# Spreading the mLSTM's rows of maxima and stabilisers by products of exact halves, and its first scores half a unit later

## The chip, the cores and the metric

The kernel runs on one core of one Trainium2 chip. The metric is device time in microseconds (us) of one execution; the kernel before takes 904.87 us, the median of three runs. Engines are named as the profile names them: PE is TensorE (PEld its loads of weights), DVE is VectorE, ACT is ScalarE, POOL is GpSimd, SP is SyncE, which issues the DMAs. L1570 is line 1570 of the kernel before.

## The reference, cut to what matters

256 tokens of width 1024 go through a first block (a gated mixer and a mixture of 32 experts) and then through two hybrid layers, each with three kinds of attention side by side. The change touches only the third kind, the mLSTM, which has 4 heads of 64 channels:

```python
m_t = jnp.maximum(inter_log, jnp.max(d_log, axis=-1))     # a running maximum for each token and head
w_intra = jnp.exp(d_log - m_t[..., None])
sc = jnp.einsum('bhtd,bhsd->bhts', qt, kt) * w_intra
num = (jnp.einsum('bhts,bhse->bhte', sc, vt) + ...)
h_t = num / jnp.maximum(jnp.abs(den), jnp.exp(-m_t))[..., None]
```

The kernel does both chunks of 128 tokens at once. With bt the running sum of the log forget gates, it keeps for each head a row of 256 tokens `rg` = input gate less bt, a row `rM` = running maximum of `rg` (from zero), and the stabiliser `rB` = bt + `rM`. Then w_intra[s, t] = exp(rg[s] - rM[t]) for s <= t, and the lower bound of the denominator is exp(-rB[t]).

## The kernel before, in words

The two hybrid layers are written as one function for each engine: `second_pe`, `second_act`, `second_dve`, `second_pool`, `second_sp`. Each is a hand-written list of steps; nothing reorders them, and the engines meet only through semaphores. The order of the lines at the end of each function is therefore the order on its engine.

The projections of a layer are cut into 22 units of 256 columns. Unit u of a layer is two `tile` steps on PE, `tile(l, u, 0)` and `tile(l, u, 1)`, each of 24 matmuls of 256 columns: 8 slices of the contraction, times 3 products. The 3 products are those of float32 numbers that have been split into two halves of type fp32r: high by high, low by high, high by low. ACT makes the high half of a unit's weights by a copy (`high(l, u)`, L1353) and DVE the low half by a subtraction (`low(l, u)`, L1361), in pieces of 128x1024. Units for values are done with the tokens as weights in `by_token` (L1495, 512 columns each, 48 matmuls for two units). SP loads the unit U when PE is done with unit U-4.

Between the tiles stand the small steps of the attentions, in plain float32. Those of the mLSTM, in PE's order:

```python
tile(l, 6, 0)
stabilisers(l)
tile(l, 6, 1)
m_rows(l, 0)
m_scores(l, 0)
tile(l, 7, 0)
m_rows(l, 1)
tile(l, 7, 1)
m_out(l, 0)
m_scores(l, 1)
```

- `gate_chain` (DVE) makes the rows `rg`, `rM`, `rB`, each 4 partitions (one a head) by 256 tokens. `s_gate` counts its steps.
- `stabilisers` (PE): two tiny matmuls that turn `rg` into columns (L1558, L1559), and two float32 matmuls that spread the rows `rB` over 64 partitions a head (L1561, L1562) by constants `selp` of zeros and ones. ACT takes exp(-.) of them in `stab_exp` (L1822).
- `m_rows(l, j)` (PE, L1570): two float32 matmuls with the constants `selm`, which spread the rows `rM` of heads 2j and 2j+1 over 128 partitions each. DVE's `m_log` (L2065, L2066) subtracts them from a mask into X1, ACT's `m_exp` (L1829) takes the exponential.
- `m_scores(l, j)` (PE, L1584): the products of keys and queries. DVE's `m_weigh` (L2074) multiplies them by X1 into X2.
- `m_out(l, j)` (PE, L1603, L1608): numerator and denominator. ACT's `m_den` (L1833) and DVE's `m_norm` (L2081, L2084, L2087) finish them.

Around these, `conv_silu` (ACT, L1806) ends the mLSTM's convolution, whose taps are DVE's (`taps`, L2008); `gate(l, "co")` (L1870) is a sigmoid; `gate_columns` (L2043) copies the columns of `rg`. Later on PE come `r_scores` (L1621), `norm_mean` (L1645) and `by_token(l, U_AV)`. `r_scores` waits for `m_norm` of heads 2 and 3, `norm_mean` for `m_gate` (L2093), and `by_token(l, U_AV)` for the low halves of the first pieces of units 10 and 11, of which the second is `low(l, 11, 0)`. The constants `selm` and `selp` lie in `late`, a tile that one DMA loads (L2455).

Of the kernel before, what the change touches and what calls it, by code (L numbers as in the profile page):

```python
# [13 lines left out]
T = 256  # L14
# [44 lines left out]
def build(nc, p, out):  # L59
    pe, act, dve, pool, sp = nc.tensor, nc.scalar, nc.vector, nc.gpsimd, nc.sync  # L60
    with ExitStack() as ctx:
        def sb(name, *shape):
            return ctx.enter_context(nc.sbuf_tensor(name, [128, *shape], F32))
# [6 lines left out]
        def overlay(**shapes):  # L70

            with ExitStack() as side:
                return [side.enter_context(nc.sbuf_tensor(n, [128, *shape], F32)) for n, shape in shapes.items()]
# [14 lines left out]
        X1 = sb("X1", 3, 384)  # L88
        rw = sb("rw", 9, 36)
        crep = sb("crep", 8, 32)  # L90
# [3 lines left out]
                                                 X2=(3, 384))  # L94
        (more,) = overlay(more=(2, 4096))
# [15 lines left out]
        def con(name, a=0, n=None):  # L111
            at, w = CONST[name]
            src, at = (cst, at) if at < EARLY else (late, at - EARLY)
            return src[:, at + a:at + (w if n is None else a + n)]
# [1138 lines left out]
        def second_block():  # L1253
# [130 lines left out]
            def root_table():  # L1384

                act.activation(trow[:, 0:1], E6, ACT.Sqrt)
# [58 lines left out]
            def second_pe():  # L1445
# [109 lines left out]
                def stabilisers(l):  # L1555
                    pe.wait_ge(s_late, 16)
                    pe.wait_ge(s_gate, 23 * l + 23)
                    pe.matmul(bank[2][:, 0:4], rg[:, 0:128], ident[0:4, 0:4], start=True, stop=True)  # L1558
                    pe.matmul(bank[2][:, 4:8], rg[:, 128:256], ident[0:4, 0:4], start=True, stop=True).then_inc(s_gcT, 1)  # L1559
                    pe.wait_ge(s_rs, 12 if l else 9)  # L1560
                    pe.matmul(bank[6][:, 0:T], con("selp", 0, 128)[0:4, :], rB, start=True, stop=True)  # L1561
                    pe.matmul(bank[6][:, T:2 * T], con("selp", 128, 128)[0:4, :], rB, start=True, stop=True).then_inc(s_stab, 1)  # L1562

                def m_rows(l, j):
                    if j:
                        pe.wait_ge(s_mW, 8 * l + 4)
                    else:
                        pe.wait_ge(s_gc, l + 1)
                    for x in range(2):
                        pe.matmul(bank[2][:, T * x:T * x + T], con("selm", 256 * j + 128 * x, 128)[0:4, :], rM,  # L1570
                                  start=True, stop=True).then_inc(s_mM, 1)
# [127 lines left out]
                for l in range(2):  # L1699
# [30 lines left out]
                    m_scores(l, 0)  # L1730
                    tile(l, 7, 0)
                    m_rows(l, 1)
                    tile(l, 7, 1)
# [60 lines left out]
            def second_act():  # L1794
# [13 lines left out]
                def gate_start(l):  # L1808
                    act.wait_ge(s_gate, 23 * l + 4)
                    act.activation(ra, rf, ACT.Abs).then_inc(s_gabs, 1)  # L1810
                    act.wait_ge(s_gabs, 2 * l + 1)
                    act.activation(re, ra, ACT.Exp, scale=-1.0).then_inc(s_gabs, 1)
# [70 lines left out]

                root_table()
                for l in range(2):
# [13 lines left out]
                    gate_start(l)  # L1899
                    for j in range(4):  # L1900
                        conv(l, j)
                    high(l, 6)
                    by_token(l, bcv, U_BV, s_bcv)
                    high(l, 7)
                    for j in range(4):
                        conv_silu(l, j)
# [89 lines left out]
            def second_dve():  # L1996
# [15 lines left out]
                def gate_chain(l):  # L2012
                    g, U = 23 * l, NU * l + U_ROWS
# [8 lines left out]
                    dve.wait_ge(s_gabs, 2 * l + 2)  # L2022
# [16 lines left out]
                    yield  # L2039

# [232 lines left out]
                for l in range(2):  # L2273
# [32 lines left out]
                    for j in range(4):  # L2306
                        take(tap[j], 1)
                    gate_columns(l)
                    low(l, 7, 0)
                    for j in range(4):  # L2310
                        take(tap[j], 1)
                    low(l, 7)
# [267 lines left out]
```

## Time and profile before

| | |
|---|---|
| time, median of 3 runs | 904.87 us (904.82 to 905.17) |
| time of the profiled execution | 905.45 us |
| its span in the profile | 904.2 us |
| PE busy | 857.6 us, 95% |
| DVE, ACT busy | 415.3 us, 300.2 us |
| TensorE clock granted | 0.99 of full speed |

The span is the time from the first to the last instruction in the profile; 1.25 us of the execution lie outside it. The first 600 us are the first block, where the experts' weights stream in; the two hybrid layers take the rest, about 152 us each. Everything that the change touches lies between 613 and 665 us (first layer) and 765 and 817 us (second layer).

### The profile page before, as it was taken

What the parts mean: (1) busy time and instruction counts of PE and PEld (TensorE: products, weight loads), DVE (VectorE), ACT (ScalarE), POOL (GpSimd) and SP (SyncE); (2) the same over time, 40 slices, a digit from 0 to 9 for tenths busy, and PEclk for the clock granted to TensorE, in tenths of its full rate; (3) what the DMA queues carried; (4) which work ended last, traced back from release to release, by engine and by line L of the source; (5) the groups of instructions that cost most, each with busy time, mean ns of one, the idle gap of its engine ahead of it and who ended that gap; (6) DMA issues with size and microseconds to landing.
All of it is one profiled execution on the core that took longest, in us unless ns stands there. A gap on an engine that the chain in (4) does not pass through costs nothing.

```text
span 904.2 us, 12189 instructions
## 1 busy us (share of the span) xinstructions
PE 857.6 (95%) x5030; PEld 552.6 (61%) x5030; DVE 415.3 (46%) x807; ACT 300.2 (33%) x542; POOL 10.3 (1%) x14
## 2 busy tenths in 40 slices
PE   5999999999998989898989899999999999999997
PEld 2668875344444334443444243498879999897995
DVE  3196954111210112011111011089798879989875
ACT  4253242111111111110111011174746666556663
POOL 0001000000000000000000000000100000010000
PEclk9999999999999999999999999999999999999999
DMA  9999989999999999999999999963425345643431
GB/s 370 426 424 428 394 349 416 399 428 428 427 427 429 428 427 426 427 429 428 427 428 428 428 422 423 392 235 140 148 87 186 141 163 190 185 137 104 178 140 71
DMA packets 34857, 292.96 MB, mean 324 GB/s; under 512 B 11376, under 2 KB 11888, under 8 KB 12912
## 3 DMA queue, kind: packets, MB, share of 16 engines
q1 hardware_dynamic: 34800, 292.16, 79.2%
q8 instruction: 41, 0.67, 0.3%
q14 instruction: 16, 0.13, 0.0%
HBM read 290.05 MB, written 1.05 MB: 322 GB/s over the span
## 4 chain that ended last, share of the span: by engine, by line
PE 72%; DMA 22%; DVE 4%; ACT 1%; issue 1%; SPq 0%; ACTq 0%
PE bank L1471 20%; PE bank L1019 16%; DMA more<-in_expert_w 14%; PE bank L1050 8%; DMA ring<-in_expert_w 7%; PE bank L1495 5%; PE bank L403 3%; PE bank L1514 2%; PE bank L950 2%; PE bank L419 2%; DVE X L373 2%; PE bank L990 2%; DMA ring<-in_ada_w 2%; PE bank L446 2%; PE bank L1662 1%; PE bank L1688 1%
## 5 line engine op out<-in xcount | busy, mean ns | idle before, releaser
L1019 PE MATMUL bank<-ring,xg 128*64 128x512 f32 x760 | 232.3, 603 | 13.9 <-DMA ring<-in_expert_w 13.9
L1471 PE MATMUL bank<-HH,halves 128*128 128x256 f32 x848 | 163.9, 289 | 0.0
L1019 PEld LDWEIGHTS bank<-ring,xg 128*64 128x64 f32 x760 | 72.7, 139 | 132.3 <-issue 105.9
L1471 PEld LDWEIGHTS bank<-HH,halves 128*128 128x128 f32 x848 | 135.4, 192 | 5.6 <-issue 4.8
L1019 PE MATMUL bank<-more,xg 128*64 128x512 f32 x256 | 116.9, 608 | 7.5 <-DMA more<-in_expert_w 7.5
L1471 PE MATMUL bank<-HL,halves 128*128 128x256 f32 x424 | 120.3, 284 | 0.0
L1137 DVE TENSOR_TENSOR X<-X,bank 128x512 f32<-128x512 f32 x16 | 11.0, 687 | 226.4 <-PE bank L1019 226.4
L1050 PE MATMUL bank<-ring,X 128*64 128x512 f32 x384 | 114.3, 596 | 0.7 <-ACT X L1090 0.7
L1361 DVE TENSOR_TENSOR halves<-raw,halves 128x1024 fp32r<-128x1024 f32 (+1 forms) x84 | 92.0, 1127 | 6.5 <-ACT halves L1353 6.4
L1150 DVE SCALAR_TENSOR_TENSOR ygL<-bank,small,ygH 128x512 fp32r<-128x512 f32 x32 | 24.0, 750 | 136.2 <-ACT ygH L1097 136.2
L1471 PEld LDWEIGHTS bank<-HL,halves 128*128 128x128 f32 x424 | 81.7, 193 | 0.8 <-issue 0.5
L1353 ACT ACTIVATE halves<-raw 128x1024 fp32r<-128x1024 f32 (+1 forms) x84 | 78.4, 978 | 5.8 <-DMA raw<-in_units 5.8
L1050 PEld LDWEIGHTS bank<-ring,X 128*64 128x64 f32 x384 | 35.1, 137 | 46.5 <-issue 43.5
L1019 PEld LDWEIGHTS bank<-more,xg 128*64 128x64 f32 x256 | 35.0, 140 | 45.8 <-issue 34.4
L1097 ACT ACTIVATE ygH<-bank,small 128x512 fp32r<-128x512 f32 x32 | 22.0, 687 | 123.2 <-PE bank L1050 123.2
L1061 ACT ACTIVATE xg<-bank,modc 128x256 f32<-128x256 f32 x32 | 13.5, 472 | 138.5 <-PE bank L950 134.4
L1050 PE MATMUL bank<-more,X 128*64 128x512 f32 x128 | 56.6, 595 | 2.1 <-DMA more<-in_expert_w 1.4
L1078 ACT ACTIVATE X<-bank 128x512 f32<-128x512 f32 x16 | 9.6, 597 | 105.4 <-PE bank L1019 105.4
L1495 PE MATMUL bank<-halves,HH 128*128 128x512 f32 x128 | 42.4, 412 | 0.0
L990 PE MATMUL bank<-PT,ygH 128*128 128x256 f32 x128 | 32.7, 293 | 0.4 <-DVE ygL L1150 0.4
L1050 PEld LDWEIGHTS bank<-more,X 128*64 128x64 f32 x128 | 16.9, 137 | 23.6 <-issue 20.0
L990 PE MATMUL bank<-PT,ygL 128*128 128x256 f32 x128 | 31.2, 281 | 0.0
(353 smaller groups left out, 1213.9 us busy)
## 6 DMA issues: line engine op xcount, KB each, us to landing
ring<-in_expert_w SPq DMA_DIRECT2D x63, 2048.0 KB, 27.0
more<-in_expert_w SPq DMA_DIRECT2D x22, 2048.0 KB, 26.3
raw<-in_units SPq DMA_DIRECT2D x38, 1024.0 KB, 5.0
ring<-in_ada_w SPq DMA_DIRECT2D x10, 2048.0 KB, 20.9
ring<-in_expert_w SPq DMA_DIRECT2D x17, 1024.0 KB, 28.1
ring<-in_w_in SPq DMA_DIRECT2D x3, 2048.0 KB, 34.9
more<-in_ada_w SPq DMA_DIRECT2D x2, 2048.0 KB, 27.6
ring<-in_w_out SPq DMA_DIRECT2D x2, 2048.0 KB, 21.6
```

Of the source, the lines that this page charges most:

```text
L373: dve.scalar_tensor_tensor(a, w[:, k, :], cs[:, k:k + 1], a, ALU.mult, ALU.add).then_inc(s_fma, 1)
L403: t = pe.matmul(ps[:, T * j:T * j + T], w[:, k, 128 * (first + j):128 * (first + j) + 128], rhs[:, k, :], start=k == 0, stop=k == 7)
L419: t = pe.matmul(bank[4 + u][:, T * j:T * j + T], w[:, k, 256 * u + 128 * j:256 * u + 128 * j + 128], hT[:, k, :], start=k == 0 and j == 0, ...
L990: t = pe.matmul(bank[ACC[a]][:, T * k:T * k + T], part(y[:, d:d + 128]), part(PT[n % 2][:, :]), start=n == 0 and k == 0 and j == 0, stop=n ...
L1019: t = pe.matmul(bank[3 + i][64 * x:64 * x + 64, :], xg[q % 2][:, k, o + 64 * x:o + 64 * x + 64], w[:, k, :], start=k == 0, stop=k == 7)
L1050: t = pe.matmul(bank[5 + a][64 * x:64 * x + 64, :], aT[:, f, 64 * x:64 * x + 64], place(at[x])[:, 4 * a + f, :], start=f == 0, stop=f == 3)
L1097: act.activation(part(ygH[:, 512 * a:512 * a + 512]), bank[5 + a][:, :], ACT.Copy, scale=weight[n % 2]).then_inc(s_ygh, 1)
L1150: dve.scalar_tensor_tensor(part(ygL[:, h]), bank[5 + a][:, :], weight[n % 2], ygH[:, h], ALU.mult, ALU.subtract).then_inc(s_ygl, 1)
L1353: act.activation(part(hi), src, ACT.Copy).then_inc(s_hi, 1)
L1361: dve.tensor_tensor(part(lo), src, hi, ALU.subtract).then_inc(s_lo, 1)
L1471: t = pe.matmul(ps[:, T * j:T * j + T], part(x[:, k, 128 * j:128 * j + 128]), part(y[:, k, :]), start=first and a == 0, stop=last and a == ...
L1495: t = pe.matmul(v3(ps[j][:, :], 2), part(x[:, k, 128 * j:128 * j + 128]), part(y), start=k == 0 and a == 0, stop=k == 7 and a == 2, skip_g ...
```

## The change

Both rows are now split as the weights are. ACT copies `rM` and `rB` into fp32r rows `rMh` and `rBh` (`row_halves`), DVE subtracts them from the rows into `rMl` and `rBl` (`row_lows`). PE spreads a row by two fp32r matmuls that add up in PSUM (`spread_row`), with fp32r copies of `selm` and `selp`, which ACT makes once, in the first layer. The spreading of the stabilisers moves from `stabilisers` to the end of `m_rows(l, 0)`. On PE, `m_scores(l, 0)` stands after `m_rows(l, 1)` and no more ahead of `tile(l, 7, 0)`. On DVE, `row_lows` stands ahead of `gate_columns`, and both pieces of `low(l, 7)` ahead of the last taps. On ACT, `row_halves` stands ahead of `conv_silu`. The new tiles lie over tiles that are dead at that time, so no memory is added. `s_gate` counts 25 instead of 23 a layer, `s_gabs` 4 instead of 2.

```diff
--- before.py
+++ after.py
@@ -85,13 +85,18 @@
         small = sb("small", 320)
         rstd = sb("rstd", T)
         longest = ctx.enter_context(nc.sbuf_tensor("longest", [128, 1], mybir.dt.int32))
-        X1 = sb("X1", 3, 384)
-        rw = sb("rw", 9, 36)
-        crep = sb("crep", 8, 32)
+        (X1,) = overlay(X1=(3, 384))
+        _, rMh = overlay(gapX1=(768,), rMh=(384,))
+        sb("bothX1", 1152)
+        rw, crep = overlay(rw=(9, 36), crep=(8, 32))
+        (selm,) = overlay(selm=(512,))
+        sb("bothrw", 580)
 
 
         late, X3, rs, spare, rt, rows, yT, X2 = overlay(late=(NCONST - EARLY,), X3=(3, 256), rs=(T,), spare=(T,), rt=(T,), rows=(1024,), yT=(8, T),
                                                  X2=(3, 384))
+        _, selp, _, _, rBh, rBl, rMl = overlay(gap_s=(NCONST - EARLY + 768 + 256,), selp=(256,), gap_r=(256 + 1024 + 2048,),
+                                               gap_X2=(256,), rBh=(256,), rBl=(256,), rMl=(384,))
         (more,) = overlay(more=(2, 4096))
         sb("both", NCONST - EARLY + 768 + 512 + 256 + 1024 + 2048 + 1152)
 
@@ -1554,21 +1559,30 @@
 
                 def stabilisers(l):
                     pe.wait_ge(s_late, 16)
-                    pe.wait_ge(s_gate, 23 * l + 23)
+                    pe.wait_ge(s_gate, 25 * l + 23)
                     pe.matmul(bank[2][:, 0:4], rg[:, 0:128], ident[0:4, 0:4], start=True, stop=True)
                     pe.matmul(bank[2][:, 4:8], rg[:, 128:256], ident[0:4, 0:4], start=True, stop=True).then_inc(s_gcT, 1)
-                    pe.wait_ge(s_rs, 12 if l else 9)
-                    pe.matmul(bank[6][:, 0:T], con("selp", 0, 128)[0:4, :], rB, start=True, stop=True)
-                    pe.matmul(bank[6][:, T:2 * T], con("selp", 128, 128)[0:4, :], rB, start=True, stop=True).then_inc(s_stab, 1)
+
+                def spread_row(ps, chosen, high, low):
+
+                    pe.matmul(ps, part(chosen), part(high[0:4, 0:T]), start=True, stop=False)
+                    return pe.matmul(ps, part(chosen), part(low[0:4, 0:T]), start=False, stop=True)
 
                 def m_rows(l, j):
                     if j:
                         pe.wait_ge(s_mW, 8 * l + 4)
                     else:
                         pe.wait_ge(s_gc, l + 1)
+                        pe.wait_ge(s_gate, 25 * l + 24)
                     for x in range(2):
-                        pe.matmul(bank[2][:, T * x:T * x + T], con("selm", 256 * j + 128 * x, 128)[0:4, :], rM,
-                                  start=True, stop=True).then_inc(s_mM, 1)
+                        h = 2 * j + x
+                        spread_row(bank[2][:, T * x:T * x + T], selm[0:4, 128 * h:128 * h + 128], rMh, rMl).then_inc(s_mM, 1)
+                    if j == 0:
+                        pe.wait_ge(s_rs, 12 if l else 9)
+                        pe.wait_ge(s_gate, 25 * l + 25)
+                        for x in range(2):
+                            t = spread_row(bank[6][:, T * x:T * x + T], selp[0:4, 128 * x:128 * x + 128], rBh, rBl)
+                        t.then_inc(s_stab, 1)
 
                 def m_scores(l, j):
                     if j:
@@ -1727,9 +1741,9 @@
                     stabilisers(l)
                     tile(l, 6, 1)
                     m_rows(l, 0)
-                    m_scores(l, 0)
                     tile(l, 7, 0)
                     m_rows(l, 1)
+                    m_scores(l, 0)
                     tile(l, 7, 1)
                     m_out(l, 0)
                     m_scores(l, 1)
@@ -1806,9 +1820,9 @@
                     act.activation(cc[:, j, :], cc[:, j, :], ACT.Silu).then_inc(s_cc, 1)
 
                 def gate_start(l):
-                    act.wait_ge(s_gate, 23 * l + 4)
+                    act.wait_ge(s_gate, 25 * l + 4)
                     act.activation(ra, rf, ACT.Abs).then_inc(s_gabs, 1)
-                    act.wait_ge(s_gabs, 2 * l + 1)
+                    act.wait_ge(s_gabs, 4 * l + 1)
                     act.activation(re, ra, ACT.Exp, scale=-1.0).then_inc(s_gabs, 1)
 
                 def by_token(l, dst, u, signal):
@@ -1880,6 +1894,13 @@
                     if l and n == 0:
                         act.wait_ge(s_unit, NU)
                     act.activation(part(flat(YH[:, k:k + 2, :])), flat(yT[:, k:k + 2, :]), ACT.Copy).then_inc(s_yh, 1)
+
+                def row_halves(l):
+
+                    act.wait_ge(s_gate, 25 * l + 22)
+                    act.activation(part(rMh[0:4, 0:T]), rM, ACT.Copy).then_inc(s_gabs, 1)
+                    act.wait_ge(s_gate, 25 * l + 23)
+                    act.activation(part(rBh[0:4, :]), rB, ACT.Copy).then_inc(s_gabs, 1)
 
                 root_table()
                 for l in range(2):
@@ -1897,11 +1918,16 @@
                         scale_root(bank[6][:, 0:2], s_st2, 2)
                         high(l, 5)
                     gate_start(l)
+                    if l == 0:
+                        act.wait_ge(s_late, 16)
+                        act.activation(part(selm[0:4, :]), con("selm")[0:4, :], ACT.Copy)
+                        act.activation(part(selp[0:4, :]), con("selp")[0:4, :], ACT.Copy)
                     for j in range(4):
                         conv(l, j)
                     high(l, 6)
                     by_token(l, bcv, U_BV, s_bcv)
                     high(l, 7)
+                    row_halves(l)
                     for j in range(4):
                         conv_silu(l, j)
                     gate(l, "co")
@@ -2010,7 +2036,7 @@
                         yield
 
                 def gate_chain(l):
-                    g, U = 23 * l, NU * l + U_ROWS
+                    g, U = 25 * l, NU * l + U_ROWS
                     dve.wait_ge(s_unit, U + 1)
                     dve.tensor_tensor(ri, unit_bank(l, U_ROWS)[0:4, 0:T], rs[0:4, :], ALU.mult).then_inc(s_gate, 1)
                     dve.tensor_tensor(rf, unit_bank(l, U_ROWS)[32:36, 0:T], rs[32:36, :], ALU.mult).then_inc(s_gate, 1)
@@ -2019,7 +2045,7 @@
                     dve.tensor_scalar(ri, ri, col("gbi", l)[0:4, :], None, ALU.add).then_inc(s_gate, 1)
                     dve.tensor_scalar(rf, rf, col("gbf", l)[0:4, :], None, ALU.add).then_inc(s_gate, 1)
                     yield
-                    dve.wait_ge(s_gabs, 2 * l + 2)
+                    dve.wait_ge(s_gabs, 4 * l + 2)
                     for _ in log1p_dve(re, ra, rw_, rv, s_gate, g + 4):
                         yield
                     dve.wait_ge(s_gate, g + 18)
@@ -2037,6 +2063,12 @@
                     dve.wait_ge(s_gate, g + 22)
                     dve.tensor_tensor(rB, rB, rM, ALU.add).then_inc(s_gate, 1)
                     yield
+
+                def row_lows(l):
+                    dve.wait_ge(s_gabs, 4 * l + 3)
+                    dve.tensor_tensor(part(rMl[0:4, 0:T]), rM, rMh[0:4, 0:T], ALU.subtract).then_inc(s_gate, 1)
+                    dve.wait_ge(s_gabs, 4 * l + 4)
+                    dve.tensor_tensor(part(rBl[0:4, :]), rB, rBh[0:4, :], ALU.subtract).then_inc(s_gate, 1)
 
                 def gate_columns(l):
                     dve.wait_ge(s_gcT, l + 1)
@@ -2305,11 +2337,11 @@
                     take(one, 1)
                     for j in range(4):
                         take(tap[j], 1)
+                    row_lows(l)
                     gate_columns(l)
-                    low(l, 7, 0)
+                    low(l, 7)
                     for j in range(4):
                         take(tap[j], 1)
-                    low(l, 7)
                     m_log(l, 0)
                     m_log(l, 1)
                     scaled(l, U_BR, br[:, 0:2, :], s_br)
```

The order on PE in the first layer, from the tiny matmuls that turn `rg` to the first `m_out`. The names are tiles: `cst` and `late` hold constants, X the rows, scr the convolved queries and keys. First the order before; the rows left out are the rest of a tile's 24 matmuls:

```order
L1559 MATMUL bank<-cst,X 128x4
L1561 MATMUL bank<-X,late 128x256
L1562 MATMUL bank<-X,late 128x256
L1471 MATMUL bank<-HH,halves 128x256
...
L1570 MATMUL bank<-X,late 128x256 x2
L1584 MATMUL bank<-scr 128x256 x2
L1584 MATMUL bank<-scr 128x128 x2
L1471 MATMUL bank<-HH,halves 128x256
...
L1570 MATMUL bank<-X,late 128x256 x2
L1471 MATMUL bank<-HH,halves 128x256
```

The same stretch of PE in the changed kernel, where L1476 is the tiles' line, L1568 and L1569 are `spread_row`, and L1598 is `m_scores`:

```order
L1564 MATMUL bank<-cst,X 128x4
L1476 MATMUL bank<-HH,halves 128x256
...
L1568 MATMUL bank<-rMh,selm 128x256
L1569 MATMUL bank<-rMl,selm 128x256
...
L1568 MATMUL bank<-rBh,selp 128x256
L1569 MATMUL bank<-rBl,selp 128x256
...
L1568 MATMUL bank<-rMh,selm 128x256
L1569 MATMUL bank<-rMl,selm 128x256
L1598 MATMUL bank<-scr 128x256 x2
L1598 MATMUL bank<-scr 128x128 x2
```

Six float32 matmuls a layer have become twelve of fp32r, and the scores have moved behind a whole tile.

DVE in the same stretch, before, from the end of the gate chain to the first `m_log`:

```order
L2038 TENSOR_TENSOR X<-X 4x256
L2211 COPY rstd<-bank 128x256
L2008 SCALAR_TENSOR_TENSOR scr<-scr,cols 128x256 x4
L2043 COPY small<-bank 128x8
L1361 TENSOR_TENSOR halves<-raw,halves 128x1024
L2008 SCALAR_TENSOR_TENSOR scr<-scr,cols 128x256 x4
L1361 TENSOR_TENSOR halves<-raw,halves 128x1024
L2065 SCALAR_TENSOR_TENSOR X<-bank,late 128x256
```

DVE in the changed kernel, where L2034 are the taps, L1366 the low halves, L2075 the copy of the columns and L2097 the first `m_log`:

```order
L2064 TENSOR_TENSOR X<-X 4x256
L2243 COPY rstd<-bank 128x256
L2034 SCALAR_TENSOR_TENSOR scr<-scr,cols 128x256 x4
L2069 TENSOR_TENSOR rMl<-X,rMh 4x256
L2071 TENSOR_TENSOR rBl<-X,rBh 4x256
L2075 COPY small<-bank 128x8
L1366 TENSOR_TENSOR halves<-raw,halves 128x1024 x2
L2034 SCALAR_TENSOR_TENSOR scr<-scr,cols 128x256 x4
L2097 SCALAR_TENSOR_TENSOR X<-bank,late 128x256
```

Two short subtractions are new, and the last four taps stand behind one more piece of 128x1024.

## Rows read from the trace of the kernel before

**Rows 1.** Busy time by stretch, the two hybrid layers (stretch, length, busy of each engine)

```profile
600.00:752.00 152.00, 152.00 (x1151) 137.41 (x1151) 129.75 (x238) 92.46 (x153) 2.93 (x4) 0.99 0.42 154
752.00:904.00 152.00, 145.87 (x1026) 127.27 (x1024) 124.28 (x222) 85.51 (x142) 2.93 (x4) 1.00 0.42 141
```

**Rows 2.** The chain that ended last, from 600 us (start, us, what)

```profile
633.06 3.06 PE bank L1471 x24
636.13 1.05 PE bank L1570 x4
...
641.10 1.06 PE bank L1570 x4
...
645.22 0.80 PE bank L1603 x8
...
660.87 1.52 PE bank L1621 x32
662.39 1.06 PE bank L1645 x2
...
721.03 31.86 PE bank L1471 x264
...
787.83 1.06 PE bank L1570 x4
```

**Rows 3.** Timeline of PE around the stabilisers (start, us, instruction)

```profile
631.96 0.67 PE L1561 MATMUL bank<-X,late 4*128 4x256 f32 x2
...
632.99 0.38 PE L1471 MATMUL bank<-HH,halves 128*128 128x256 f32 x1
```

**Rows 4.** Timeline of ACT (in brackets idle time before, and its releaser)

```profile
613.12 0.42 ACT L1810 ACTIVATE X<-X 4x256 f32<-4x256 f32 x1 [2.91 <-DVE X L2020]
...
631.91 1.28 ACT L1806 ACT_TABLE_LOAD   x1
634.16 1.61 ACT L1806 ACTIVATE scr<-scr 128x256 f32<-128x256 f32 x4 [0.97 <-DVE scr L2008]
...
639.52 1.49 ACT L1829 ACTIVATE X<-X,small 128x256 f32<-128x256 f32 x4
...
644.18 1.99 ACT L1353 ACTIVATE halves<-raw 128x1024 fp32r<-128x1024 f32 x2
646.74 0.38 ACT L1833 ACTIVATE scr<-bank 128x256 f32<-128x256 f32 x1 [0.57 <-PE bank L1608]
```

**Rows 5.** Timeline of SP: the issue of the load of the constants

```profile
592.79 0.65 SPq L2455 DMA_DIRECT2D late<-in_cst  x1
```

**Rows 6.** DMA view of that stretch: the same load, its size and us from issue to landing

```profile
late<-in_cst SPq DMA_DIRECT2D x1, 1536.0 KB, 14.8
```

**Rows 7.** Timeline of DVE

```profile
630.20 0.41 DVE L2038 TENSOR_TENSOR X<-X 4x256 f32<-4x256 f32 x1
...
630.87 1.65 DVE L2008 SCALAR_TENSOR_TENSOR scr<-scr,cols 128x256 f32<-128x256 f32 x4
...
637.30 0.42 DVE L2065 SCALAR_TENSOR_TENSOR X<-bank,late 128x256 f32<-128x256 f32 x1 [0.85 <-PE bank L1570]
...
640.41 1.25 DVE L2074 SCALAR_TENSOR_TENSOR X<-bank,X 128x384 f32<-128x384 f32 x2 [1.37 <-ACT X L1829]
642.25 0.42 DVE L2065 SCALAR_TENSOR_TENSOR X<-bank,late 128x256 f32<-128x256 f32 x1 [0.59 <-PE bank L1570]
...
647.56 1.02 DVE L2074 SCALAR_TENSOR_TENSOR X<-bank,X 128x384 f32<-128x384 f32 x2 [1.89 <-PE bank L1584]
...
649.09 0.41 DVE L2081 TENSOR_TENSOR scr<-scr,rows 128x256 f32<-128x256 f32 x1
...
659.46 0.42 DVE L2087 TENSOR_TENSOR scr<-bank,scr 128x256 f32<-128x256 f32 x1
...
661.53 1.22 DVE L1361 TENSOR_TENSOR halves<-raw,halves 128x1024 fp32r<-128x1024 f32 x1
...
791.94 1.25 DVE L2074 SCALAR_TENSOR_TENSOR X<-bank,X 128x384 f32<-128x384 f32 x2 [1.19 <-ACT X L1829]
```

## The prediction

> **What bounds the kernel now.** I read the busy time by stretch first. In the first hybrid layer PE is busy for all of 152 us, and in the second until the closing steps, at a clock of 0.99 to 1.00 of full speed [rows 1]: 2.4 GHz, the upper of its two levels. DVE is busy for 130 us of the 152, ACT for 92. The chain that ended last says the same: from 600 us to the closing steps it is PE alone, one piece behind the other. So PE's own work sets the end, a microsecond taken from it is a microsecond won, but only as long as PE never waits. Today it never does. The second question is therefore how late the others may be. For that I read the timelines of DVE and ACT beside PE's: at which time DVE ends the work that a PE step waits for, and when PE comes there.
>
> **What goes on PE.** A float32 matmul of 4x256 costs 1.05 / 2 = 0.53 us in the two steps of rows of maxima (1.05 and 1.06) [rows 2]. The two stabiliser matmuls run from 631.96 to 632.99, 1.03 us [rows 3]. A layer loses 1.03 + 1.05 + 1.06 = 3.14 us.
>
> **What comes on PE.** Twelve fp32r matmuls of 256 columns. A long run of tiles has 264 of them in 31.86 us, 0.121 each [rows 2], load of weights hidden. Those have 128 partitions of input, the new ones 4; the float32 ones with 4 partitions are the nearest row, and at 0.53 they stand to 0.121 as 4.4 to 1. I take 0.121, since only the columns seem to count: 12 x 0.121 = 1.45 us. There is one more small term: 24 matmuls of a tile between two float32 steps take 3.06 us, not 24 x 0.121 = 2.90 [rows 2], so a float32 step costs 0.16 at its two edges. Before there were three such steps in this stretch of a layer, after there are two (the tiny turns, and the scores). PE's work falls by 3.14 - 1.45 + 0.16 = 1.85 us a layer, 3.7 in all. That is the ceiling. The bounds of a product of halves are 0 (then 3.3 a layer) and 0.53 (rival C).
>
> The Trainium skill (FP8 and Floating Point Precision, TensorE Precision Notes) says that true float32 takes four passes through the array. By that rule a float32 spread would be 4 x 0.121 = 0.48, a layer's gain 1.45, and the ceiling 2.9 us instead of 3.7. The trace has 4.4 passes' worth; the row decides.
>
> **The new work on ACT and DVE, first layer.** The copies of `selm` and `selp` follow the gate's exponential at 615.3, once. ACT takes 0.42 us for 4x256 [rows 4], so I put 1.1 us on the two. ACT then idles for over 9 us until PE's values are there at 628.7, and that idle time hides it; without it a tap would be 1 us late. They wait for `late`, which is issued at 592.79 [rows 5] and lands 14.8 later [rows 6], 607.6: 7 us of slack.
>
> `row_halves` runs on ACT in front of the table load at 631.91. The rows are there (`rB` ends at 630.61 [rows 7]), the copies take about 0.75 together, to 632.66. The load ends later by that, at 634.0, but it waited 0.97 us for the taps anyway [rows 4]. Hidden.
>
> DVE: the four taps end at 632.45. Then the two subtractions, 0.41 each at most [rows 7], to 633.2, the copy of the columns (0.1), both pieces of `low(7)` (1.15 apart), to 635.5, and the last four taps (1.6), to 637.1. PE comes to the products at 635.0 and to `tile(7, 0)` at 636.0; columns and pieces are ready for both. PE's second rows need `m_log` of heads 0 and 1, four instructions behind the taps: 638.2, and PE comes at 638.9. Ready too, with 0.6 us.
>
> **What is late next.** The taps. Their last one ended at 635.3 and let the Silus end at 635.77 [rows 4]; now they end at 637.55, and all that ACT does next, two table loads included, shifts by 1.8 us. The exponentials `m_exp` go from 639.52 to 641.3 [rows 4], `m_weigh` from 640.41 to 642.2, its second ends 643.45 [rows 7]. PE wants it for `m_out(0)`. That step stood at 645.22 [rows 2] and can now start at 645.22 - 1.85 = 643.35. A wait of about 0.15 us: so the late scores fit, just. Behind it on PE stand `m_scores(1)` and `tile(8, 0)`.
>
> **Where the gain is cut.** DVE goes on: `m_log` of heads 2 and 3 starts at 643.4 instead of 642.25. To the end of `low(8)` it took 3.4 us before (647.56 less 1.89 of waiting, less 642.25 [rows 7]), so 646.8. There DVE used to wait 1.89 us for PE's second scores until 647.56; these are now done near 645.8. It starts `m_weigh` at 646.8 and `m_norm` at 646.8 + (649.09 - 647.56) = 648.3, against 649.09. ACT must have made the denominator: its copy of unit 9 shifts by 1.8 and ends near 648.0, `m_den` (0.38 [rows 4]) at 648.3. Both agree: **DVE is 0.8 us ahead, PE 1.7 to 1.85**. From 649.09 on DVE has no idle time for 38 us, so it can't catch up more; PE gains on it.
>
> Three PE steps now wait for that DVE run: `r_scores` (660.87 [rows 2]) for `m_norm`, which ends at 659.88 [rows 7]: slack 0.99. `norm_mean` (662.39) for the gate, which ends about 661.6: 0.8. The values of unit 10 and 11 (662.39 + 1.06 = 663.45) for the piece that ends at 661.53 + 1.22 = 662.75 [rows 7]: 0.70, the least. I take 0.25 of it off for the semaphore and a load of weights, as estimate (the bounds are 0 and 0.6). So PE may run ahead by 0.8 + 0.45 = 1.25 us there, and the rest of its gain, 0.6 us, turns into a wait. Later DVE waits for PE for microseconds, so both shift together and the 1.25 is kept to the end.
>
> The second layer is 787.83 - 636.13 = 151.70 us later on PE [rows 2], but `m_weigh` at 791.94 only 151.53 [rows 7]: DVE and ACT are 0.17 us earlier there. Its gain is 1.25 + 0.17 = 1.42.
>
> **The sum.** 1.25 + 1.42 = 2.67 us. The profiled execution took 905.45, so 902.8 by its own time. It stood 0.58 us over the median of 904.87; from the median, 902.2. What a measurement of this kernel can tell from no change is about 0.2%, 1.8 us.
>
> **Rivals.**
> A: all of PE's gain reaches the end, because DVE and ACT run tighter than I lay them out (1.85 ahead, not 0.8). For it: ACT's idle times; against it: DVE has none in that stretch. 904.87 - 3.7 = 901.2. Chance 0.15.
> B: DVE does not get ahead at all, because `m_den` on ACT, behind two table loads and four pieces, is as late as PE's scores were. Then only the slack counts: 0.45 + 0.62 = 1.1 us, 903.8. Chance 0.2.
> C, slower: a product of halves with 4 partitions isn't cheap. It decides from (3.14 + 0.16) / 12 = 0.275 us each; at the 0.53 of the float32 row a layer would have 12 x 0.53 = 6.4 instead of 3.3, 6 us lost in both layers: 911. Against it: partitions do not show in the float32 rows. Chance 0.07.
> D: the work goes, the time doesn't: the wait for values needs the piece before PE's queue comes to their weights, so its slack is 0.1 and not 0.45, and DVE stays where it was. 0.1 + 0.3 us, 904.5. Chance 0.13.
> The forecast itself: 0.45, with 901.7 to 902.9 as its own range.
>
> **How the numbers follow.** The time is the forecast's, 902.2. The range has to take in A (901.2) and most of B, up to 904.1; out of it are C, D and B's upper edge, some 0.2. Faster by over 0.2% is under 903.06: the forecast, A, and a small part of B (0.07), 0.67. Within it: the rest of B and D, 0.26. Slower: C, 0.07.
>
> **What the profile after would show.** Right: 48 fp32r rows for spreading near 0.12 us apart; `m_out(0)` near 643.4 in the first layer; a small idle time of PE there and one of 0.4 to 0.6 us at the values, `norm_mean` or `r_scores`; DVE's wait before the second pair of `m_weigh` gone; the last taps ending near 637.1, and `m_norm` starting 0.8 earlier. Wrong: no idle time of PE at all (A), `m_norm` at 649 (B), products 0.3 us apart or more (C). The second layer should show the same, shifted. What I can't see in this trace is the cost of fp32r with 4 partitions, and how early PE must know that a piece is there.

## The result and the profile after

The changed kernel took 903.04 us (median of 16 runs), the kernel before 905.31 beside it. The ratio is 0.9973, with a 95% interval from 0.9964 to 0.9982: 2.4 us faster, where 2.67 were forecast. The forecast of 902.2 us was reckoned from 904.87 for the kernel before, which took 905.31 here. The profiled execution took 903.23 us.

Single executions of either kernel differ by more than the effect (904.49 to 908.49 us for the kernel before), and in the profiles of this document the first turns of `rg` start anywhere from 630.12 to 634.84 us. A stretch inside the profile, behind the first block, is steadier, so I compare the kernels by the time from the turns of `rg` in the first layer (L1558, now L1563) to the first matmul of the second layer's output projection (L1514, now L1519). PE's timeline of the kernel before has its two ends at:

```profile
631.49 0.38 PE L1558 MATMUL bank<-cst,X 4*128 4x4 f32 x2
...
875.63 0.63 PE L1514 MATMUL bank<-halves,YH 128*128 128x512 f32 x2
```

and that of the changed kernel at:

```profile
631.67 0.38 PE L1563 MATMUL bank<-cst,X 4*128 4x4 f32 x2
...
873.70 0.63 PE L1519 MATMUL bank<-halves,YH 128*128 128x512 f32 x2
```

That is 244.14 us before and 242.03 after, 2.11 us less. All that the change touches lies in it. The granted clock of TensorE is 1.00 from 635 to 870 us in every profile of this document, so no difference there comes from the clock. "+12.36" below means 12.36 us behind the turns of that layer. All such figures are differences of rounded times; 0.01 between two of them is rounding.

The chain that ended last goes from end to end of the pieces, so that its starts lie up to 0.17 us behind those of a timeline. Of the kernel before (beside [rows 2]):

```profile
631.56 0.31 PE bank L1558 x2
...
663.45 2.75 PE bank L1495 x12
```

and of the changed kernel:

```profile
631.74 0.31 PE bank L1563 x2
632.05 0.22 PE bank L1564 x2
632.27 3.06 PE bank L1476 x24
635.33 0.31 PE bank L1568
...
636.47 3.06 PE bank L1476 x24
639.53 0.31 PE bank L1568
...
640.19 0.85 PE bank L1598 x8
641.04 3.06 PE bank L1476 x24
644.10 0.80 PE bank L1617 x8
...
661.28 0.10 issue
661.37 1.10 PE bank L1659 x2
662.50 3.00 PE bank L1500 x12
...
812.12 1.06 PE bank L1659 x2
813.17 2.79 PE bank L1500 x12
```

The block of eight products takes 636.47 - 635.33 = 1.14 us, the block of four 0.66. The first product of each takes 0.31, not 0.12, and the tile behind a block still 3.06. So `m_out(0)` comes 12.36 us behind the turns (644.10 - 631.74) instead of 13.66 (645.22 - 631.56): 1.30 us won, in both layers. There is no wait in front of it. Later the first layer loses 0.43 of this again: 0.14 around `norm_mean` (L1659), in front of which 0.10 us pass that the chain calls "issue" (DVE's gate, L2125, ends at 661.22, and the loads of weights for `norm_mean` begin at 661.34), and 0.29 at the values (L1500), with 3.00 us for 12 matmuls where the kernel before had 2.75, and 0.04 in front of them. The second layer has 2.79 there.

The busy time by stretch (compare [rows 1]) still has PE near the full length, with 0.7 us missing in the first layer's 152 us, 0.6 of it in one wait that ends at 608.16 us, before anything that the change touches:

```profile
600.00:752.00 152.00, 151.28 (x1166) 137.37 (x1165) 132.26 (x243) 94.61 (x159) 2.96 (x4) 1.00 0.43 158
```

DVE in the same stretch (compare [rows 7]):

```profile
632.64 0.41 DVE L2069 TENSOR_TENSOR rMl<-X,rMh 4x256 fp32r<-4x256 f32 x1
...
635.65 1.65 DVE L2034 SCALAR_TENSOR_TENSOR scr<-scr,cols 128x256 f32<-128x256 f32 x4
...
642.40 1.25 DVE L2106 SCALAR_TENSOR_TENSOR X<-bank,X 128x384 f32<-128x384 f32 x2 [3.43 <-ACT X L1843]
...
648.46 0.42 DVE L2113 TENSOR_TENSOR scr<-scr,rows 128x256 f32<-128x256 f32 x1
...
655.33 0.42 DVE L2085 TENSOR_TENSOR scr<-scr 128x256 f32<-128x256 f32 x1
655.89 0.42 DVE L2088 TENSOR_TENSOR scr<-scr 128x256 f32<-128x256 f32 x1
...
661.14 1.22 DVE L1366 TENSOR_TENSOR halves<-raw,halves 128x1024 fp32r<-128x1024 f32 x1
```

`m_weigh` now waits 3.4 us for ACT. Its idle time ahead of the second pair of `m_weigh` is gone. This layer's turns are 0.18 us later in this execution, so `m_norm` at 648.46 is 0.81 us ahead of before. Between the last L2085 and L2088, at the end of the rotation, 0.56 us pass instead of the 0.33 to 0.34 between its neighbours, and no view names what DVE waited for. After it DVE is 0.57 ahead only: its piece for the values ends at 662.36, 30.69 behind the turns, instead of 662.75 [rows 7], 31.26 behind them.

ACT (compare [rows 4]):

```profile
631.96 0.40 ACT L1901 ACTIVATE rMh<-X 4x256 fp32r<-4x256 f32 x1
632.26 0.40 ACT L1903 ACTIVATE rBh<-X 4x256 fp32r<-4x256 f32 x1
632.68 1.28 ACT L1820 ACT_TABLE_LOAD   x1
636.15 1.61 ACT L1820 ACTIVATE scr<-scr 128x256 f32<-128x256 f32 x4 [2.19 <-DVE scr L2034]
...
641.51 1.48 ACT L1843 ACTIVATE X<-X,small 128x256 f32<-128x256 f32 x4
```

The two copies cost nothing; the Silus wait for the later taps.

### The profile page after: what moved, and what is told of

It reads as the page before. It is cut to its first block, busy times and chain, and to the rows that moved or that the text cites. A ratio compares the mean times of both kernels' runs of the same rounds, so it can differ in the third digit from the quotient of the medians.

```text
span 901.9 us, 12203 instructions
## 1 busy us (share of the span) xinstructions
PE 855.3 (95%) x5030; PEld 550.6 (61%) x5030; DVE 416.6 (46%) x811; ACT 301.7 (33%) x548; POOL 10.3 (1%) x14
## 3 DMA queue, kind: packets, MB, share of 16 engines
HBM read 290.05 MB, written 1.05 MB: 323 GB/s over the span
## 4 chain that ended last, share of the span: by engine, by line
PE 71%; DMA 22%; DVE 4%; ACT 1%; issue 1%; SPq 0%; ACTq 0%
PE bank L1476 20%; PE bank L1024 16%; DMA more<-in_expert_w 14%; PE bank L1055 8%; DMA ring<-in_expert_w 7%; PE bank L1500 5%; PE bank L408 3%; PE bank L1519 2%; PE bank L955 2%; PE bank L424 2%; DVE X L378 2%; PE bank L995 2%; DMA ring<-in_ada_w 2%; PE bank L451 2%; PE bank L1676 1%; PE bank L1702 1%
## 5 line engine op out<-in xcount | busy, mean ns | idle before, releaser
L1024 PE MATMUL bank<-ring,xg 128*64 128x512 f32 x760 | 229.4, 607 | 14.2 <-DMA ring<-in_expert_w 14.2
L1476 PE MATMUL bank<-HH,halves 128*128 128x256 f32 x848 | 162.8, 288 | 0.0
L1476 PEld LDWEIGHTS bank<-HH,halves 128*128 128x128 f32 x848 | 134.5, 191 | 4.5 <-issue 3.5
L1024 PE MATMUL bank<-more,xg 128*64 128x512 f32 x256 | 113.8, 594 | 7.2 <-DMA more<-in_expert_w 7.2
L1476 PE MATMUL bank<-HL,halves 128*128 128x256 f32 x424 | 119.9, 283 | 0.0
L1366 DVE TENSOR_TENSOR halves<-raw,halves 128x1024 fp32r<-128x1024 f32 (+1 forms) x84 | 91.9, 1129 | 6.2 <-ACT halves L1358 6.2
L1476 PEld LDWEIGHTS bank<-HL,halves 128*128 128x128 f32 x424 | 81.2, 191 | 0.7 <-issue 0.5
L1500 PE MATMUL bank<-halves,HH 128*128 128x512 f32 x128 | 41.8, 408 | 0.0
```

The costliest lines, as they stand in the source:

```text
L1024: t = pe.matmul(bank[3 + i][64 * x:64 * x + 64, :], xg[q % 2][:, k, o + 64 * x:o + 64 * x + 64], w[:, k, :], start=k == 0, stop=k == 7)
L1366: dve.tensor_tensor(part(lo), src, hi, ALU.subtract).then_inc(s_lo, 1)
L1476: t = pe.matmul(ps[:, T * j:T * j + T], part(x[:, k, 128 * j:128 * j + 128]), part(y[:, k, :]), start=first and a == 0, stop=last and a == ...
L1500: t = pe.matmul(v3(ps[j][:, :], 2), part(x[:, k, 128 * j:128 * j + 128]), part(y), start=k == 0 and a == 0, stop=k == 7 and a == 2, skip_g ...
```

## The experiments

Each is compared with the kernel before by its ratio, and by the stretch of its profile. The sums:

| run | stretch, us | m_out(0), layer 1 / 2 | ratio (95% interval) |
|---|---|---|---|
| before | 244.14 | +13.66 / +13.66 | 1 |
| the change | 242.03 | +12.36 / +12.36 | 0.9973 (0.9964 to 0.9982) |
| halves_only | 241.92 | +12.64 / +12.46 | 0.9974 (0.9962 to 0.9986) |
| move_only | 244.14 | +13.66 / +13.66 | 1.0012 (0.9998 to 1.0026) |
| dve_order | 241.57 | +12.37 / +12.37 | 0.9965 (0.9949 to 0.9981) |
| high_only | 241.97 | +12.03 / +11.86 | 0.9974 (0.9960 to 0.9988) |
| k128 | 241.78 | +12.05 / +11.86 | 0.9981 (0.9968 to 0.9995) |
| pool_rope | 241.58 | +12.37 / +12.37 | 0.9972 (0.9961 to 0.9982) |
| k128_order | 240.47 | +11.81 / +11.81 | 0.9964 (0.9947 to 0.9980) |
| best2 | 240.49 | +11.81 / +11.81 | 0.9960 (0.9945 to 0.9975) |
| best3 | 240.20 | +11.82 / +11.62 | 0.9958 (0.9942 to 0.9974) |
| f32_k128 | 242.77 | +12.97 / +12.97 | one run, no interval |

The intervals are up to 0.17% wide to each side, so the ratios tell the versions from before, but hardly from each other; for that the stretch has to serve, one profile each.

**The two parts apart.** `halves_only` is the changed kernel with the first scores and DVE's order put back:

```diff
                     m_rows(l, 0)
+                    m_scores(l, 0)
                     tile(l, 7, 0)
                     m_rows(l, 1)
-                    m_scores(l, 0)
...
-                    low(l, 7)
+                    low(l, 7, 0)
                     for j in range(4):
                         take(tap[j], 1)
+                    low(l, 7)
```

> The change without its move: rows split and spread by halves, the first scores and DVE's order of taps and low halves left where they stood before. My theory: PE saves 12 x 0.12 us against 3.14 us less about 0.35 us of edges a layer; the taps end 0.75 us later than before because of the two subtractions, the Silus near 636.7 in the first layer, and PE asks for its scores at 636.5, so it waits 0.2 to 0.4 us there. PE is then 1.0 us ahead at the first m_out, DVE 0.9 ahead: gain 0.9 to 1.0 us a layer, about 1.9 us in all, ratio 0.998, only a few tenths behind the full change. Rival: the move is what makes the halves pay, and without it the wait for the Silus eats the gain (1.3 us a layer): ratio 0.9995 to 1.001.

`move_only` is the kernel before with the scores moved:

```diff
                     m_rows(l, 0)
-                    m_scores(l, 0)
                     tile(l, 7, 0)
                     m_rows(l, 1)
+                    m_scores(l, 0)
```

> The kernel before with only the first scores moved behind the second rows of maxima, all in float32. My theory: no PE work changes; m_weigh of head 0 waits for the scores until 643.1 instead of 640.4, DVE reaches the second pair of m_weigh about 0.1 us later than PE's second scores, so nothing reaches the end: ratio 1.000 within 0.0003, at most 0.3 us slower. Rival: the late scores delay m_out by over 0.5 us a layer, ratio 1.001 or more.

The move alone changes nothing, to the hundredth, in the stretch; the ratio's interval holds 1. The halves alone give 2.22 us, no less than the full change's 2.11. The wait for the Silus (ACT's L1820) is there, but short; PE's timeline of `halves_only`:

```profile
636.82 0.92 PE L1598 MATMUL bank<-scr 64*128 64x256 f32 x8 [0.21 <-ACT scr L1820]
```

So all of the gain comes from the products. The move with its order of DVE takes away that wait of 0.21 us in the first layer and puts a larger one at the values. Both rivals are out: for the halves by the ratio and the stretch, for the move by the profile alone, where `m_out(0)` stands at +13.66 as before (its ratio of 1.0012 could not have decided it).

**What limits the gain.** `dve_order` puts only DVE's order back (the lower half of the first diff above):

> The changed kernel with DVE's old order: the second piece of low(7) behind the last taps again. My theory (the first layer's gain is cut because PE has to wait 0.4 us for DVE's pieces at norm_mean and at the values): Silus, exponentials and m_weigh come 1.1 us earlier, DVE is 1.2 us ahead instead of 0.8, the 0.4 us wait in the first layer goes, the second layer stays: 0.3 to 0.5 us faster than the changed kernel, ratio to the kernel before 0.9968. Rival (PE's own work is the limit in both layers): same as the changed kernel, 0.9973, and no shorter wait in the trace.

`high_only` leaves the low halves of the rows out of the products, and with them part of the rows' precision:

```diff
-                    pe.matmul(ps, part(chosen), part(high[0:4, 0:T]), start=True, stop=False)
-                    return pe.matmul(ps, part(chosen), part(low[0:4, 0:T]), start=False, stop=True)
+                    return pe.matmul(ps, part(chosen), part(high[0:4, 0:T]), start=True, stop=True)
```

> The changed kernel, which spreads only the high halves and leaves the low ones out: 12 matmuls fewer, 0.72 us less on PE a layer; ACT and DVE do what they did. It leaves out part of the computation. My theory (DVE bounds what PE can gain, with 0 to 0.05 us of slack left in either layer): at most 0.2 us faster than the changed kernel, ratio 0.9971 to 0.9973, with PE idle for about 0.7 us more a layer ahead of r_scores, norm_mean and the values. Rival (PE bound): 1.4 us faster, ratio 0.9957.

`pool_rope` lets POOL do the last two steps of the rotation:

```diff
+                    if i:
+                        c = 8 * l + 4
+                        pool.wait_ge(s_rope, c + 2)
+                        pool.wait_ge(s_ropp, 4 * l + 4)
+                        pool.tensor_tensor(bt[:, a, :], bt[:, a, :], tmp4[:, a, :], ALU.subtract).then_inc(s_rope, 1)
+                        pool.tensor_tensor(bt[:, a + 1, :], bt[:, a + 1, :], tmp4[:, a + 1, :], ALU.add).then_inc(s_rope, 1)
...
+                    if i:
+                        return
```

> The changed kernel with the last two of the eight rotation steps ahead of r_scores moved from DVE to POOL. My theory: DVE is 0.67 us quicker there, and 0.2 more in the first layer, where it waited for POOL, so m_norm, the gate and the low half of unit 11 come that much earlier; PE's wait at norm_mean and the values goes in both layers. From the turns of rg to the output projection PE takes 241.5 us instead of 242.03 (before 244.14): 0.5 us faster than the changed kernel. Rival: POOL slows DVE by working beside it, or its rotation comes too late for r_scores: no gain.

With twelve matmuls fewer in the two layers, `high_only` wins 0.06 us in the stretch, not 1.4: PE gives it all back in waits. Its timeline of PE shows two of them, which the changed kernel does not have, for `m_weigh` and for `m_norm`:

```profile
642.15 0.87 PE L1616 MATMUL bank<-X,scr 128*64 128x256 f32 x8 [0.31 <-DVE X L2105]
...
658.09 1.59 PE L1634 MATMUL bank<-scr 32*128 32x256 f32 x32 [0.22 <-DVE scr L2118]
```

`dve_order` and `pool_rope` do not touch PE's work, and win 0.46 and 0.45 us, both almost all in the first layer. Both make DVE's run ahead of the values earlier or shorter: its piece for the values ends 30.20 and 29.96 us behind the turns in the first layer, against 30.69. (POOL beside it does slow DVE: the first step of `m_norm` takes 0.58 us in `pool_rope` instead of 0.41. The steps taken away are worth more.) Together the three show that DVE cut the gain, by 0.4 us in the first layer, and that the second layer had next to nothing to lose.

How much slack PE needs can be read at the values. The loads of weights (PEld) of the kernel before and of the changed kernel, the first of the values in the first layer:

```profile
662.86 0.19 PEld L1495 LDWEIGHTS bank<-halves,HH 128*128 128x128 f32 x1 [0.24 <-issue]
```

```profile
662.47 0.30 PEld L1500 LDWEIGHTS bank<-halves,HH 128*128 128x128 f32 x2 [0.84 <-issue]
```

Before, the load ran while the float32 matmuls of `norm_mean` (662.39 to 663.45 [rows 2]) were still going. After, DVE's piece ended at 661.14 + 1.22 = 662.36, the load began 0.11 us later, when `norm_mean` was done, and nothing hid it. In `dve_order` the load began at 662.04, 0.35 us ahead of `norm_mean`'s end at 662.39 (661.34 + 1.05), and the 12 matmuls took 2.76, next to nothing lost.

DVE bounds the second layer too, though less. The same piece there, before and after:

```profile
813.24 1.22 DVE L1361 TENSOR_TENSOR halves<-raw,halves 128x1024 fp32r<-128x1024 f32 x1
```

```profile
811.59 1.22 DVE L1366 TENSOR_TENSOR halves<-raw,halves 128x1024 fp32r<-128x1024 f32 x1
```

The turns of that layer start at 783.20 and 782.51, so the piece ends 31.26 and 30.30 behind them: DVE is 0.96 ahead, and PE loses 0.04 at the values. This is why `high_only`, whose `m_out(0)` comes 0.5 us earlier there, wins no more than 0.06.

**The edges.** The products came out at 0.12 us each, but the blocks did not. `k128` takes them over 128 partitions:

```diff
-                    pe.matmul(ps, part(chosen), part(high[0:4, 0:T]), start=True, stop=False)
-                    return pe.matmul(ps, part(chosen), part(low[0:4, 0:T]), start=False, stop=True)
+                    pe.matmul(ps, part(chosen), part(high[:, 0:T]), start=True, stop=False)
+                    return pe.matmul(ps, part(chosen), part(low[:, 0:T]), start=False, stop=True)
...
-                    act.activation(part(rMh[0:4, 0:T]), rM, ACT.Copy).then_inc(s_gabs, 1)
+                    act.activation(part(rMh[:, 0:T]), X3[:, 2, :], ACT.Copy).then_inc(s_gabs, 1)
...
+                pool.wait_ge(s_late, 16)
+                pool.memset(X3[:, :, :], 0.0).then_inc(s_late, 1)
```

> The changed kernel with the spreading products taken over 128 partitions instead of 4: ACT copies and DVE subtracts all 128 partitions of the rows' tile, whose other partitions POOL has set to zero once, and the constants are copied whole. My theory: what a small step costs at its edges comes from the change in the number of input partitions, not from float32; so the first block of products (8) falls from 1.14 to 0.97 us and the second starts 0.1 us sooner, 0.27 us a layer less on PE. The first layer is bounded by DVE and gains nothing, the second at most 0.05: time as the changed kernel's within 0.1 us. Rival: the edges belong to the float32 steps, or to every change of tiles, and the block of 8 still takes 1.14 us.

`k128_order` adds DVE's old order:

> Products over 128 partitions, and DVE's old order of taps and low halves (the order alone took 241.57 us from the turns to the output projection). My theory: the 0.27 us a layer of the edges now reach PE's stream at the first m_out in both layers (12.10 us behind the turns instead of 12.37), but in the first layer DVE cuts it again at the values: 241.2 us in all. Rival (edges are not those of the partitions): 241.57, m_out at 12.37.

and `f32_k128` does the same to the kernel before, in float32, without halves and without the move:

```diff
-                        pe.matmul(bank[2][:, T * x:T * x + T], con("selm", 256 * j + 128 * x, 128)[0:4, :], rM,
+                        pe.matmul(bank[2][:, T * x:T * x + T], con("selm", 256 * j + 128 * x, 128), X3[:, 2, :],
...
+                pool.memset(X3[:, :, :], 0.0).then_inc(s_late, 1)
```

> The kernel before, with its six float32 spreading matmuls a layer taken over 128 partitions (the rows' other partitions set to zero once by POOL), the turns of rg left at 4. My theory: an edge of 0.19 us is paid where the number of input partitions changes between two PE steps, whatever their type. The float32 step of rows standing alone between two tiles has two such edges, and both go; of the other two steps an edge only moves to the neighbour with few partitions. Per layer 0.37 us less, 243.4 us from the turns to the output projection instead of 244.14; the matmuls themselves still 0.53 us. Rival: the edge belongs to the step from fp32r to float32; then 244.14 stays.

The chain of `k128_order`:

```profile
634.69 0.12 PE bank L1568
634.81 0.12 PE bank L1569
...
635.64 2.88 PE bank L1476 x24
638.52 0.12 PE bank L1568
```

and that of `f32_k128`, whose second and fifth lines are steps of rows in float32 (the third is `m_scores`):

```profile
633.03 2.86 PE bank L1471 x24
635.90 0.87 PE bank L1570 x4
636.76 0.85 PE bank L1584 x8
637.62 3.06 PE bank L1471 x24
640.68 0.87 PE bank L1570 x4
641.54 2.87 PE bank L1471 x24
```

The 0.19 us are gone from the first product, and 0.18 from the tile behind: the edge is paid where the number of input partitions changes, in fp32r and in float32 alike. It is not one of few partitions alone: the tile behind the scores, which have 64, still takes 3.06 in `f32_k128` (fourth line). My theory had the cause right and the size too small: 0.56 us a layer in the changed kernel, 0.69 in the one before, where 0.27 and 0.37 were expected. The size of one edge held, their number did not: padding removes three such changes a layer in either kernel (the rows' change to the scores only becomes one from 128 to 64), and 3 x 0.19 = 0.57. What the other 0.12 of the kernel before are, no run shows.

Without the edges a float32 spread costs 0.87 / 2 = 0.435 us. At 128 partitions the halves should then save 6 x 0.435 - 12 x 0.121 = 1.16 us a layer, and they do (+12.97 against +11.81). What is left of the 1.30 measured is 0.69 - 0.56 = 0.13, the unexplained part of the kernel before; it is a difference of the same figures and checks nothing.

`k128` alone won 0.25 us in the stretch: 0.04 in the second layer, as expected, and 0.21 in the first, where DVE bounds it. There DVE's last L2085 and L2088 (its L2088 and L2091) stand 0.34 us apart again, 0.22 less than in the changed kernel, and I put the gain down to that; it was not tested by itself. (The span of this profile is 904.9 us, by its first block; the stretch leaves that out.) With DVE's order the full 0.56 a layer arrive, where I had expected another cut at the values.

**All together.** `best2` is `k128_order` with `pool_rope`, `best3` is `k128_order` with the turns of `rg` over 128 partitions too:

```diff
-                    pe.matmul(bank[2][:, 0:4], rg[:, 0:128], ident[0:4, 0:4], start=True, stop=True)
+                    pe.matmul(bank[2][:, 0:4], X3[:, 1, 0:128], ident[:, 0:4], start=True, stop=True)
```

> All three: products over 128 partitions, DVE's old order, the last rotation steps on POOL. My theory: nothing is in PE's way any more in this stretch, so all of PE's saving reaches the end: 1.30 + 0.27 = 1.57 us a layer, 244.14 - 3.14 = 241.0 us from the turns to the output projection, ratio to the kernel before 0.9965. Rival: another wait of DVE or ACT appears at once and keeps it at 241.5.

> Products over 128 partitions and DVE's old order (240.47 us from the turns to the output projection), and the two tiny turns of rg over 128 partitions too. My theory: the turns' two edges go, 0.37 us a layer, 239.7 us if no wait of DVE takes it back, the tile behind them 2.9 us instead of 3.06; ratio to the kernel before 0.995. Rival: DVE's run from m_weigh to the values, 0.25 us from being the limit in the first layer, cuts it: 240.2.

`best2` ends where `k128_order` does (240.49 and 240.47): with the old order POOL's help has nothing left to remove. `best3` wins 0.19 us more at the second layer's `m_out(0)` and nothing at the first's, where 0.37 a layer were expected. The other 0.08 us of its 240.20 lie ahead of the second layer's turns: the tile in front of them takes 2.87 us instead of 2.96 there, and in the first layer too, where the stretch does not count it. The rival had named 240.2, but for a cut at the values, and that is not where the first layer lost it. The chain and the timeline of DVE in `best3`:

```profile
635.65 3.06 PE bank L1476 x24
```

```profile
635.75 1.21 DVE L1366 TENSOR_TENSOR halves<-raw,halves 128x1024 fp32r<-128x1024 f32 x1
```

`tile(7, 0)` took 3.06 there instead of 2.88: its second half of weights is the piece that DVE ended at 636.96, and PE, now earlier, wanted it at 635.65 + 12 x 0.12 = 637.1, too soon for the load to be hidden, as I read it. `best3` is the fastest by its stretch, 3.94 us less than the kernel before and 1.83 less than the change; by its ratio, 0.9958, it beats the kernel before, and its interval overlaps the change's.

## Why the prediction was right, point by point

- **PE's saving** (forecast 1.85 us a layer, measured 1.30): the term that was mis-sized. The products cost 0.121 each as said. But the two blocks that the change brought have edges of their own, 1.14 - 8 x 0.121 = 0.17 and 0.66 - 4 x 0.121 = 0.18, which I put at nothing, and the two edges that I credited (0.16) did not go: that is 0.51 of the 0.55. I had put the edges down to the float type, and they go by the partitions, so that a change of partitions goes on being paid when the type changes. My 0.53 for a float32 spread held an edge as well; the matmul itself is 0.435. That partitions do not show in the float32 rows was wrong. The Trainium skill's rule of four passes (FP8 and Floating Point Precision, TensorE Precision Notes), 4 x 0.121 = 0.48, would have been nearer to the 0.435 than the row that I let decide.
- **The new work on ACT and DVE**: hidden, as said. The copies 631.96 to 632.66, the subtractions to 633.4, the last taps to 637.3 (forecast 637.1, and these turns are 0.18 later). The changed kernel has 24 products in all, 12 a layer; the 48 rows that I announced were a slip.
- **The wait at `m_out(0)`** (0.15 forecast): none. `m_weigh` ended at 643.65, but PE came 0.55 us later than forecast, by the smaller saving. It appears when PE is faster (`high_only`, 0.31).
- **DVE 0.8 us ahead at `m_norm`**: 0.81. But 0.22 of it was lost at L2088 in the rotation. That is no wait for POOL, whose last product ended at 650.2, 5 us earlier. The pause stands at the same instruction in the first layer of `halves_only`, `dve_order` and `high_only`, at four different times, and neither there in the kernel before nor in `k128` and `k128_order`, which have one more wait on DVE. So it seems to go with the program and not with the state of the other engines; its cause stays open.
- **The cut at the values**: the right place for two thirds of it; the rest, 0.14, was lost one step earlier, at `norm_mean`. In the first layer the lead allowed to PE was forecast as 0.8 + 0.45 = 1.25; it was 0.57 for DVE, and the first layer's gain in the stretch, 0.87, leaves 0.30 for the slack. In the second it was forecast as 1.42, that is 0.97 for DVE and 0.45 of slack; DVE was 0.96 ahead, and with the same 0.30 this gives 1.26, where 1.24 were gained. So the slack was mis-sized by 0.15 in both layers, and DVE's lead by the pause in the first.
- **The sum**: 1.25 + 1.42 = 2.67 forecast, 0.87 + 1.24 = 2.11 in the stretch. The 2.4 us of the ratio hold 2.11 in their interval (1.6 to 3.3 us).
- **The rivals**: A (all 3.7 us) is out, B too (DVE did get ahead). C is out: the products are cheap at 4 partitions, at 0.121. D's mechanism was partly right: the load of weights wants its piece early, but DVE did move, so its 904.5 did not come.

The way of reckoning held: what is won is the smaller of PE's saving and the lead that DVE allows. Nearly all of the 0.56 us between forecast and stretch are the slack (0.15 in each layer) and the pause (0.22). That the larger error, 0.55 us a layer in PE's saving, did not show in the time is luck: PE's own 1.30 still lay just above what DVE allowed, by 0.04 in the second layer.

## What to carry to other kernels

Where one engine runs without a gap, a microsecond taken from it is only won up to the slack of the engines that feed it; taking away further work (here twelve matmuls) shows at once whether that slack is used up. A row of a small step between large ones holds its edges, so compare the neighbours' lengths too before you price a replacement by it, and ask whether the replacement will have the same edges. Small matmuls over few partitions between full ones may be cheaper when padded with zeros to the same partitions as their neighbours.

## What the runs showed of the hardware

A change in the number of input partitions between two groups of matmuls (128 to 4 and back) cost about 0.19 us each time, in fp32r and in float32 (`k128_order` and `f32_k128` against the change and before); at 128 partitions throughout, a float32 step between fp32r tiles cost none of it (tile 2.86 instead of 3.06 us). A float32 matmul of 256 columns took 0.435 us, 3.6 times one of fp32r, both with 4 and with 128 partitions of input once its edges are set apart. A load of weights that waited for DVE began 0.11 us behind the end of DVE's instruction (662.36 to 662.47), and cost PE about 0.3 us when no longer matmul covered it. A DVE step of 128x256 took 0.58 us instead of 0.41 with POOL at work beside it (`pool_rope`).
